# Value tiles of a gated recurrence brought to token layout by block transposes and transfers instead of TensorE transposes

## The chip, the cores and the metric

The kernel runs on one core of a Trainium2 chip. The metric is the device time of one execution in microseconds (us). A core has five engines that run their own instruction streams and meet at semaphores: PE (TensorE, matrix products into PSUM), DVE (VectorE), ACT (ScalarE), POOL (GpSimd) and SP (SyncE, which here only issues transfers). ACT issues transfers too, on a queue of its own.

## The reference

One layer of a hybrid encoder on 512 tokens of width 1024: a SwiGLU block, then a mixer with attention and a bidirectional gated recurrence side by side, then a second SwiGLU block. All in float32. The part that matters here:

```python
h = rmsnorm(x, mix_norm_g[l])
aq, ak, av, hq, hff, hfb, hi, hg, ga, gb = split_columns(h @ w_in[l])
y_attn = axial_gqa_attention(aq, ak, av, ...) @ w_branch_attn[l]
y_hgrn = hgrn2_bidirectional(hq, hff, hfb, hi, hg, ...) @ w_branch_hgrn[l]

# in the recurrence, v = hi, 8 heads of 64 channels, chunks of 32 tokens:
o_intra = einsum('bhnts,bhnse->bhnte', scores, v)
contrib = einsum('bhnsd,bhnse->bhnde', k * exp(b_last - b), v)
```

`hi` (the recurrence's values, 512 channels) comes out of the projection with channels on partitions, four tiles of 128 channels by 512 tokens. The two products above contract over tokens, so they want the values with tokens on partitions.

## The kernel before

The kernel is written out by hand for each engine, with semaphores between them; nothing is scheduled by a tool. Weights stream through in units of 128x1024 (512 KB). For a unit SP loads `raw` (two slots), ACT copies it to `w_hi` in the matmul's rounded type, DVE subtracts to get `w_lo` (four slots), and PE makes 24 matmuls of 128x512 (eight input tiles, each hi*hi, hi*lo and lo*hi) into one PSUM bank, alternating between two. DVE then evacuates the bank, multiplying by the token's norm factor `rs`.

The projection stage runs over `PROJ`, a list of 26 such units: attention v and k, four of q, then (before) four value tiles `hi`, four forget tiles `hf`, and so on. Every engine has a loop over this list with the same index i, and does in iteration i:

- PE (lines 1356 to 1379): unit i, once its weights are split (three units ahead) and the bank is read (unit i-2 evacuated). Behind the unit of a value tile, four transposes of 128x128 of `v_tmp` into PSUM bank 7 (line 1371). Then, from i = 9 on, the scores of attention item q = i - 9 (line 1329, two matmuls), which wait for `p_done` of item q-1.
- DVE (lines 1000 to 1037): for i from 10 on the reciprocal of the last item's sums; the evacuation of unit i (line 1026), for a value tile into `v_tmp`; from i = 9 on `attention_step` (line 967): block transposes of item q-1's probabilities (lines 962 and 965), then the two maxima of item q (line 974); then the split `w_lo` of unit i+3.
- ACT (lines 587 to 624): the scaling of item q-1's probabilities (line 564), the copy `w_hi` of unit i+3 (line 430), behind a value tile the copy of bank 7 to `v_h` (line 618), and the two exponentials of item q (line 558), which wait for the maxima.
- SP (lines 280 to 298): the weight loads, the swapped halves for the rotary embedding, and at i = 13 to 16 the transfers that replicate attention's v (line 295).

There is one `v_tmp` tile. Before, the attention value tile (i = 0) and the four `hi` tiles (i = 6 to 9) all go through it and through PE's transposes. `v_h` holds the result and is read first by `contributions(0)` of the recurrence (line 1449), after the projection stage. PE waits there for `vn_done`, the count of copies. Block transposes on DVE exchange rows and columns inside each 32x32 block; to bring the blocks themselves to their places, the kernel moves them by transfers. It does this already for x in the second SwiGLU block (`x_to_tokens`, line 448, issued by ACT).

Of the kernel before, what the change touches and what calls it, by code (L numbers as in the profile page):

```python
# [29 lines left out]
ACT = mybir.ActivationFunctionType  # L30
AX = mybir.AxisListType

P = 128
# [23 lines left out]
for _name, _count, _width in STREAMS:  # L57
# [3 lines left out]

PROJ = ([("av", 0), ("ak", 0)] + [("aq", t) for t in range(4)] + [("hi", t) for t in range(4)]
        + [("hf", h) for h in range(4)] + [("hq", t) for t in range(4)]
        + [("hf", h) for h in range(4, HH)] + [("hg", t) for t in range(4)])
V_TILES = {i: w for w, i in enumerate(i for i, (kind, _) in enumerate(PROJ) if kind in ("av", "hi"))}
FIRST_ITEM = 9
BLOCK = 32
BLOCKS = S // BLOCK  # L70
# [24 lines left out]
def build(nc, xT_in, up1, down1, proj, gates, branch, wout, up2, down2, mix_const, small_const, gains, gain_row, lb_logits, x_spill, out):  # L95


    with ExitStack() as ctx:
# [3 lines left out]
        def sem(name):  # L102
            return ctx.enter_context(nc.semaphore(name))
# [109 lines left out]
        lb_loaded, lb_exp, lb_ready = sem("lb_loaded"), sem("lb_exp"), sem("lb_ready")  # L213
        proj_read = sem("proj_read")
        vt_done, vn_done = sem("vt_done"), sem("vn_done")
        qsq_done, qms_done, qeps_done, qr_done = sem("qsq_done"), sem("qms_done"), sem("qeps_done"), sem("qr_done")
        cos_done = sem("cos_done")
        qn_done, rope_done = sem("qn_done"), sem("rope_done")
# [192 lines left out]
        def _(act):  # L411
# [138 lines left out]
                    split_hi(2)  # L550
            ffn(1)

            def exp_scores(q):
                for a in range(2):
                    act.wait_ge(nm_done, 2 * q + 1 + a)
                    if q:
                        act.wait_ge(pt_done, TURNS * q if a else TURNS * (q - 1) + 1)
                    A(prob[:, a, :], ps[:, 2 + a, :], ACT.Exp, bias=neg_max[:, q, a:a + 1],  # L558
                      accum_out=prob_sum[:, q, a:a + 1]).then_inc(p_done, 1)
# [27 lines left out]
            for i, (kind, t) in enumerate(PROJ):  # L587
                if i == 2:

                    act.wait_ge(lb_ready, 1)  # L590
                    A(lbt[:], lbt[:], ACT.Exp).then_inc(lb_exp, 1)
                if 3 <= i <= 7:
                    m = i - 3
                    act.wait_ge(qms_done, m + 1)
                    if m:
                        act.wait_ge(qn_done, m)
                    A(q_ms[:], ps[:, 4, :], ACT.Copy, bias=EPS).then_inc(qeps_done, 1)
                    act.wait_ge(qeps_done, m + 1)
                    A(q_rs[:], q_ms[:], ACT.Ln).then_inc(act_seq, 1)
                    act.wait_ge(act_seq, m + 1)  # L600
                    A(q_rs[:], q_rs[:], ACT.Exp, scale=-0.5).then_inc(qr_done, 1)
                if 0 <= i - FIRST_ITEM - 1 < ITEMS:
                    normalize_probs(i - FIRST_ITEM - 1)
                for n in {0: (0, 1), 1: ()}.get(i, (i,)):
                    split_hi(base + n + AHEAD)
                if i == 0:
                    rms_estimate(1)
                if kind in ("ak", "aq"):
                    m = i - 1
                    act.wait_ge(proj_read, i + 1 + BANK_CREDIT)  # L610
                    if m:
                        act.wait_ge(qms_done, m)
                    A(q_sq[:], qk[:, m, :], ACT.Square).then_inc(qsq_done, 1)
                w = V_TILES.get(i - 1)
                if w is not None:
                    act.wait_ge(vt_done, w + 1)
                    vt = ps[:, 7, :].rearrange("p (a b) -> p a b", b=P)
                    A(v_a[:] if w == 0 else v_h[:, :, P * (w - 1):P * w], vt, ACT.Copy).then_inc(vn_done, 1)
                q = i - FIRST_ITEM
                if q == Y_AT:  # L620
                    y_hi(0)
                    y_hi(1)
                if 0 <= q < ITEMS:
                    exp_scores(q)
            gate_base = BASE["gates"]


# [147 lines left out]
        def _(dve):  # L775
# [191 lines left out]
            def attention_step(q):  # L967

                if 0 <= q - 1 < ITEMS:
                    prob_blocks(q - 1)  # L970
                if 0 <= q < ITEMS:
                    for a in range(2):
                        dve.wait_ge(s_done, 2 * q + 1 + a)
                        V.reduce_max(neg_max[:, q, a:a + 1], ps[:, 2 + a, :], AX.X, negate=True).then_inc(nm_done, 1)  # L974
# [25 lines left out]
            for i, (kind, t) in enumerate(PROJ):  # L1000
                if i == 2:
                    lower_bound()
                if 3 <= i <= 7:
                    m = i - 3
                    dve.wait_ge(qr_done, m + 1)
                    link(newton(q_rs[:], q_ms[:], q_t[:]))
                    stt(qk[:, m, :], qk[:, m, :], gain[:, 33:34] if m == 0 else gq8[:], q_rs[:],
                        ALU.mult, ALU.mult).then_inc(qn_done, 1)
                    dve.wait_ge(qn_done, m + 1)
                if 0 <= i - FIRST_ITEM - 1 < ITEMS:  # L1010
                    inverse_sums(i - FIRST_ITEM - 1)
                if i != 1 and i < FIRST_ITEM:
                    split_lo(base + i + AHEAD)
                if i == 0:
                    split_lo(base + 1 + AHEAD)
                    rms_factor(1)
                if i - FIRST_ITEM == Y_AT:
                    y_lo(0)
                    y_lo(1)
                w = V_TILES.get(i)  # L1020
                if w:
                    dve.wait_ge(vt_done, w)
                dst = {"av": v_tmp[:], "hi": v_tmp[:], "ak": qk[:, 0, :], "aq": qk[:, min(1 + t, 4), :], "hf": forget[:, t, :],
                       "hq": hq[:, t % 4, :], "hg": hgate[:, t % 4, :]}[kind]
                dve.wait_ge(unit_done, base + i + 1 + W_CREDIT)
                tt(dst, ps[:, i % 2, :], rs[:], ALU.mult).then_inc(proj_read, 1)
                if 4 <= i <= 8:
                    m = i - 4
                    dve.wait_ge(mix_loaded, 16)
                    dve.wait_ge(qswap_done[m % 2], 64 * (m // 2 + 1))  # L1030
                    link(tt(q_t[:], q_swap[m % 2][:], c["sin"], ALU.mult))
                    dve.wait_ge(cos_done, m + 1)
                    tt(qk[:, m, :], q_cos[:, m % 2, :], q_t[:], ALU.add).then_inc(rope_done, 1)
                    dve.wait_ge(rope_done, m + 1)
                attention_step(i - FIRST_ITEM)
                if i >= FIRST_ITEM:
                    split_lo(base + i + AHEAD)
# [156 lines left out]
        def _(pe):  # L1194
# [137 lines left out]
            def weighted(w):  # L1332
                if w == 0:
                    pe.wait_ge(vrep_loaded, 16 * 2 * QUADS * QUADS)
                    pe.wait_ge(qeps_done, 5)
                    pe.wait_ge(vn_done, 5)
                else:
                    pe.wait_ge(yalo_done, 2 * w)
                pe.wait_ge(pt_done, TURNS * GROUP * (w + 1))
                for j in range(BLOCKS):  # L1340
                    piece = PIECE_OF[j]
                    for i in range(QUADS):
                        keys = slice(BLOCK * i, BLOCK * (i + 1))
                        for a, rows in enumerate(head_rows):
                            probs = prob_t1[piece][keys, j - PROB_PIECES[piece][0], :, :] if a else prob_t0[keys, j, :, :]
                            ins = T.matmul(ps[rows, Y_BANK + i, GROUP * BLOCK * w:GROUP * BLOCK * (w + 1)], v_rep[j // 8][keys, j % 8, rows],  # L1346
                                           probs.rearrange("p s c -> p (s c)"), start=j == 0, stop=j == BLOCKS - 1)
                ins.then_inc(pv_done, 1)
# [90 lines left out]
            def contributions(u):  # L1439
                pe.wait_ge(kn_done, u + 1)  # L1440
                if u == 0:
                    pe.wait_ge(vn_done, 5)
                if u >= 3:
                    pe.wait_ge(oeps_done, (u - 1) // 2)
                for n in range(NSUP):
                    j, tokens = n // 2, head_rows[n % 2]
                    for a, rows in enumerate(head_rows):
                        h = u // 2 * 2 + a
                        ins = T.matmul(ps[rows, 6 + n % 2, 0:S // 2].rearrange("p (e j) -> p e j", j=ST)[:, :, j],  # L1449
                                       k_nat[tokens, j, HD * a:HD * (a + 1)], v_h[tokens, j, HD * h:HD * (h + 1)], start=True, stop=True)  # L1450
                ins.then_inc(con_done, 1)
# [160 lines left out]
```

## Time and profile before

| | |
|---|---|
| median of 3 runs | 1132.91 us (lowest 1132.46) |
| the profiled execution | 1132.66 us |
| its span in the trace | 1130.9 us |
| PE busy | 1122.2 us, 99% of the span |
| PE weight loads (overlap PE) | 908.6 us, 80% |
| DVE busy | 628.8 us, 56% |
| ACT busy | 442.5 us, 39% |
| POOL busy | 81.5 us, 7% |
| chain that ended last | PE 98% |

The span is the time in the trace from the first to the last instruction; 1.8 us lie around it. One run of the three took 2531.6 us; it is left out. The chain that ended last is followed back from the last instruction, at each step to what released it. Matmuls overlap in the pipeline, so that the duration of one (0.39 us) is longer than its share (24 of them and the scores take 6.74 us).

### The profile page before, as it was taken

What the parts mean: (1) busy time and instruction counts of PE and PEld (TensorE: products, weight loads), DVE (VectorE), ACT (ScalarE), POOL (GpSimd) and SP (SyncE); (2) the same over time, 40 slices, a digit from 0 to 9 for tenths busy, and PEclk for the clock granted to TensorE, in tenths of its full rate; (3) what the DMA queues carried; (4) which work ended last, traced back from release to release, by engine and by line L of the source; (5) the groups of instructions that cost most, each with busy time, mean ns of one, the idle gap of its engine ahead of it and who ended that gap; (6) DMA issues with size and microseconds to landing.
All of it is one profiled execution on the core that took longest, in us unless ns stands there. A gap on an engine that the chain in (4) does not pass through costs nothing.

```text
span 1130.9 us, 16616 instructions
## 1 busy us (share of the span) xinstructions
PE 1122.2 (99%) x6359; PEld 908.6 (80%) x6359; DVE 628.8 (56%) x840; ACT 442.5 (39%) x658; POOL 81.5 (7%) x72
## 2 busy tenths in 40 slices
PE   9999999999999999999999999999999999999997
PEld 7888888888888777777788888888888888888886
DVE  6755555563332586647688767655555555542223
ACT  6423232232222444546856655534232323331223
POOL 0000000000000130000143320020000000000000
PEclk9999999999999999999999999999999999999999
DMA  6332322333322434212221222422244343332321
GB/s 198 124 111 75 111 92 93 108 113 103 103 95 74 172 110 133 75 57 75 76 79 57 74 76 93 168 93 93 79 126 121 91 120 108 119 110 93 99 88 75
DMA packets 51650, 114.78 MB, mean 101 GB/s; under 512 B 21904, under 2 KB 25104, under 8 KB 51344
## 3 DMA queue, kind: packets, MB, share of 16 engines
q1 hardware_dynamic: 32752, 105.16, 28.1%
q10 hardware_dynamic: 18848, 8.92, 2.7%
q8 instruction: 35, 0.57, 0.2%
q14 instruction: 15, 0.12, 0.0%
HBM read 105.41 MB, written 4.19 MB: 97 GB/s over the span
## 4 chain that ended last, share of the span: by engine, by line
PE 98%; DMA 1%; DVE 0%; ACT 0%; ACTq 0%; issue 0%; DVEq 0%
PE ps L1203 27%; PE ps L1205 27%; PE ps L1204 27%; PE ps L1229 4%; PE ps L1228 4%; PE ps L1230 4%; PE ps L1329 1%; PE ps L1346 1%; PE ps L1473 1%; DMA xT<-xT_dram 1%; PE ps L1466 0%; PE ps L1427 0%; PE ps L1449 0%; PE ps L1378 0%; PE ps L1416 0%; DMA raw<-up_dram 0%
## 5 line engine op out<-in xcount | busy, mean ns | idle before, releaser
L1203 PE MATMUL ps<-h_hi,w_hi 128*128 128x512 f32 x1024 | 407.3, 398 | 0.5 <-DVE w_lo L786 0.5
L1205 PE MATMUL ps<-h_hi,w_lo 128*128 128x512 f32 x1024 | 399.1, 390 | 0.0
L1204 PE MATMUL ps<-h_lo,w_hi 128*128 128x512 f32 x1024 | 398.8, 389 | 0.0
L786 DVE TENSOR_TENSOR w_lo<-raw,w_hi 128x1024 fp32r<-128x1024 f32 (+2 forms) x190 | 233.4, 1231 | 176.8 <-ACT w_hi L430 170.6
L430 ACT ACTIVATE w_hi<-raw 128x1024 fp32r<-128x1024 f32 (+1 forms) x182 | 194.7, 1080 | 182.8 <-PE ps L1205 74.3
L1203 PEld LDWEIGHTS ps<-h_hi,w_hi 128*128 128x128 f32 x1024 | 192.2, 188 | 55.8 <-issue 15.2
L1204 PEld LDWEIGHTS ps<-h_lo,w_hi 128*128 128x128 f32 x1024 | 192.3, 188 | 41.7 <-issue 2.9
L1205 PEld LDWEIGHTS ps<-h_hi,w_lo 128*128 128x128 f32 x1024 | 192.2, 188 | 40.6
L502 ACT ACTIVATE g_hi<-un 128x512 fp32r<-128x512 f32 (+1 forms) x44 | 27.8, 632 | 219.9 <-DVE un L786 219.9
L786 DVE TENSOR_TENSOR un<-ps,rs 128x512 f32<-128x512 f32 x44 | 30.4, 690 | 97.6 <-PE ps L1205 97.6
L1229 PE MATMUL ps<-w_hi,g_lo 128*128 128x512 f32 x176 | 68.5, 389 | 0.0
L1205 PE MATMUL ps<-g_hi,w_lo 128*128 128x512 f32 x176 | 68.5, 389 | 0.0
L1203 PE MATMUL ps<-g_hi,w_hi 128*128 128x512 f32 x176 | 68.5, 389 | 0.0
L1228 PE MATMUL ps<-w_hi,g_hi 128*128 128x512 f32 x176 | 68.5, 389 | 0.0
L1230 PE MATMUL ps<-w_lo,g_hi 128*128 128x512 f32 x176 | 68.5, 389 | 0.0
L1204 PE MATMUL ps<-g_lo,w_hi 128*128 128x512 f32 x176 | 68.5, 389 | 0.0
L786 DVE TENSOR_TENSOR g_lo<-un,g_hi 128x512 f32 (+1 forms) x44 | 30.5, 692 | 36.7 <-ACT g_hi L502 36.7
L438 ACT ACTIVATE sq<-xT 128x512 f32 (+1 forms) x16 | 10.1, 632 | 81.0 <-DVE xT L789 81.0
L558 ACT ACTIVATE prob<-ps,neg_max 128x512 f32<-128x512 f32 x32 | 21.7, 685 | 46.5 <-DVE neg_max L974 46.5
L1228 PEld LDWEIGHTS ps<-w_hi,g_hi 128*128 128x128 f32 x176 | 33.0, 188 | 6.9
L1205 PEld LDWEIGHTS ps<-g_hi,w_lo 128*128 128x128 f32 x176 | 33.0, 188 | 6.9
L1204 PEld LDWEIGHTS ps<-g_lo,w_hi 128*128 128x128 f32 x176 | 33.0, 188 | 6.9
(232 smaller groups left out, 1140.6 us busy)
## 6 DMA issues: line engine op xcount, KB each, us to landing
raw<-up_dram SPq DMA_DIRECT2D x86, 512.0 KB, 3.3
raw<-proj_dram SPq DMA_DIRECT2D x26, 512.0 KB, 3.3
raw<-down_dram SPq DMA_DIRECT2D x16, 704.0 KB, 4.0
raw<-down_dram SPq DMA_DIRECT2D x22, 512.0 KB, 3.3
raw<-gates_dram SPq DMA_DIRECT2D x16, 512.0 KB, 3.3
raw<-branch_dram SPq DMA_DIRECT2D x8, 512.0 KB, 3.3
raw<-wout_dram SPq DMA_DIRECT2D x8, 512.0 KB, 3.3
x_spill_dram<-xT ACTq DMA_DIRECT2D x1, 2048.0 KB, 7.1
```

The source lines that it names most:

```text
L430: A(w_hi[:, cst % 4, 0:width], raw[:, cst % 2, 0:width], ACT.Copy).then_inc(hi_done, 1)
L502: A(g_hi[:, 2 * it + q, :], un[:], ACT.Copy).then_inc(ghi_done, 1)
L558: A(prob[:, a, :], ps[:, 2 + a, :], ACT.Exp, bias=neg_max[:, q, a:a + 1], accum_out=prob_sum[:, q, a:a + 1]).then_inc(p_done, 1)
L786: return V.tensor_tensor(out, a, b, op)
L1203: T.matmul(ps[:, bank, :], w_hi[:, slot, cols], moving_hi(j), start=start and j == 0, stop=False)
L1204: T.matmul(ps[:, bank, :], w_hi[:, slot, cols], moving_lo(j), start=False, stop=False)
L1205: ins = T.matmul(ps[:, bank, :], w_lo[:, slot, cols], moving_hi(j), start=False, stop=stop and j == tiles - 1)
L1228: T.matmul(ps[:, bank, :], g_hi[:, j, rows], w_hi[:, slot, cols], start=first, stop=False)
L1229: T.matmul(ps[:, bank, :], g_lo[:, j, rows], w_hi[:, slot, cols], start=False, stop=False)
L1230: ins = T.matmul(ps[:, bank, :], g_hi[:, j, rows], w_lo[:, slot, cols], start=False, stop=end)
L1329: T.matmul(ps[:, 2 + a, :], qk[rows, 1 + t, P * qt:P * (qt + 1)], qk[rows, 0, :], start=True, stop=True).then_inc(s_done, 1)
L1346: ins = T.matmul(ps[rows, Y_BANK + i, GROUP * BLOCK * w:GROUP * BLOCK * (w + 1)], v_rep[j // 8][keys, j % 8, rows], probs.rearrange("p s c ...
```

## The change

Three things change together. The order of `PROJ`: the first four forget tiles now come at i = 6 to 9 and the value tiles at i = 10 to 13. The way of the value tiles to `v_h`: DVE transposes `v_tmp` in place by blocks of 32x32 (it waits for its own evacuation first), and ACT issues sixteen transfers, each of 32 partitions by four runs of 32 elements (16 KB), into `v_h`, behind the exponentials of its iteration. And the waits: the evacuation of the next value tile into `v_tmp` now waits until all transfers of the last have landed (`vh_loaded`), and PE's waits for `vn_done` of the value tiles become one wait for `vh_loaded` ahead of `contributions(0)`. PE's four groups of transposes and ACT's four copies are gone; attention's value tile keeps its own.

```diff
--- before.py
+++ after.py
@@ -61,10 +61,11 @@
 
 
 
-PROJ = ([("av", 0), ("ak", 0)] + [("aq", t) for t in range(4)] + [("hi", t) for t in range(4)]
-        + [("hf", h) for h in range(4)] + [("hq", t) for t in range(4)]
+PROJ = ([("av", 0), ("ak", 0)] + [("aq", t) for t in range(4)] + [("hf", h) for h in range(4)]
+        + [("hi", t) for t in range(4)] + [("hq", t) for t in range(4)]
         + [("hf", h) for h in range(4, HH)] + [("hg", t) for t in range(4)])
-V_TILES = {i: w for w, i in enumerate(i for i, (kind, _) in enumerate(PROJ) if kind in ("av", "hi"))}
+V_TILES = {0: 0}
+HI_AT = PROJ.index(("hi", 0))
 FIRST_ITEM = 9
 BLOCK = 32
 BLOCKS = S // BLOCK
@@ -213,6 +214,7 @@
         lb_loaded, lb_exp, lb_ready = sem("lb_loaded"), sem("lb_exp"), sem("lb_ready")
         proj_read = sem("proj_read")
         vt_done, vn_done = sem("vt_done"), sem("vn_done")
+        vblk_done, vh_loaded = sem("vblk_done"), sem("vh_loaded")
         qsq_done, qms_done, qeps_done, qr_done = sem("qsq_done"), sem("qms_done"), sem("qeps_done"), sem("qr_done")
         cos_done = sem("cos_done")
         qn_done, rope_done = sem("qn_done"), sem("rope_done")
@@ -550,6 +552,14 @@
                     split_hi(2)
             ffn(1)
 
+            def values_to_tokens(w):
+                act.wait_ge(vblk_done, w + 1)
+                blocks = v_tmp[:].rearrange("p (t j c) -> p t j c", j=QUADS, c=BLOCK)
+                for quad in range(QUADS):
+                    for to in range(QUADS):
+                        act.dma_start(v_h[BLOCK * to:BLOCK * (to + 1), :, P * w + BLOCK * quad:P * w + BLOCK * (quad + 1)],
+                                      blocks[BLOCK * quad:BLOCK * (quad + 1), :, to, :]).then_inc(vh_loaded, 16)
+
             def exp_scores(q):
                 for a in range(2):
                     act.wait_ge(nm_done, 2 * q + 1 + a)
@@ -615,13 +625,15 @@
                 if w is not None:
                     act.wait_ge(vt_done, w + 1)
                     vt = ps[:, 7, :].rearrange("p (a b) -> p a b", b=P)
-                    A(v_a[:] if w == 0 else v_h[:, :, P * (w - 1):P * w], vt, ACT.Copy).then_inc(vn_done, 1)
+                    A(v_a[:], vt, ACT.Copy).then_inc(vn_done, 1)
                 q = i - FIRST_ITEM
                 if q == Y_AT:
                     y_hi(0)
                     y_hi(1)
                 if 0 <= q < ITEMS:
                     exp_scores(q)
+                if kind == "hi":
+                    values_to_tokens(t)
             gate_base = BASE["gates"]
 
 
@@ -1017,9 +1029,8 @@
                 if i - FIRST_ITEM == Y_AT:
                     y_lo(0)
                     y_lo(1)
-                w = V_TILES.get(i)
-                if w:
-                    dve.wait_ge(vt_done, w)
+                if kind == "hi":
+                    dve.wait_ge(*((vh_loaded, 16 * QUADS * QUADS * t) if t else (vt_done, 1)))
                 dst = {"av": v_tmp[:], "hi": v_tmp[:], "ak": qk[:, 0, :], "aq": qk[:, min(1 + t, 4), :], "hf": forget[:, t, :],
                        "hq": hq[:, t % 4, :], "hg": hgate[:, t % 4, :]}[kind]
                 dve.wait_ge(unit_done, base + i + 1 + W_CREDIT)
@@ -1032,6 +1043,9 @@
                     dve.wait_ge(cos_done, m + 1)
                     tt(qk[:, m, :], q_cos[:, m % 2, :], q_t[:], ALU.add).then_inc(rope_done, 1)
                     dve.wait_ge(rope_done, m + 1)
+                if kind == "hi":
+                    dve.wait_ge(proj_read, i + 1 + BANK_CREDIT)
+                    V.transpose(v_tmp[:], v_tmp[:]).then_inc(vblk_done, 1)
                 attention_step(i - FIRST_ITEM)
                 if i >= FIRST_ITEM:
                     split_lo(base + i + AHEAD)
@@ -1333,7 +1347,7 @@
                 if w == 0:
                     pe.wait_ge(vrep_loaded, 16 * 2 * QUADS * QUADS)
                     pe.wait_ge(qeps_done, 5)
-                    pe.wait_ge(vn_done, 5)
+                    pe.wait_ge(vn_done, 1)
                 else:
                     pe.wait_ge(yalo_done, 2 * w)
                 pe.wait_ge(pt_done, TURNS * GROUP * (w + 1))
@@ -1439,7 +1453,7 @@
             def contributions(u):
                 pe.wait_ge(kn_done, u + 1)
                 if u == 0:
-                    pe.wait_ge(vn_done, 5)
+                    pe.wait_ge(vh_loaded, 16 * QUADS * QUADS * 4)
                 if u >= 3:
                     pe.wait_ge(oeps_done, (u - 1) // 2)
                 for n in range(NSUP):
```

On ACT, in the projection loop around the value tiles. Before, iterations 9 and 10 from the weight copy of the one to the exponentials of the other (`v_h` is the copy of the transposed tile out of PSUM, `prob` the attention item's probabilities):

```order
L430 ACTIVATE w_hi<-raw 128x1024 [waits unit_done,raw_loaded0]
L618 ACTIVATE v_h<-ps 128x4x128 [waits vt_done]
L558 ACTIVATE prob,prob_sum<-ps,neg_max 128x512 [waits nm_done] x2
L564 ACTIVATE prob<-prob,inv_sum 128x512 [waits inv_done]
L564 ACTIVATE prob<-prob,inv_sum 128x512
L430 ACTIVATE w_hi<-raw 128x1024 [waits unit_done,raw_loaded1]
L618 ACTIVATE v_h<-ps 128x4x128 [waits vt_done]
L558 ACTIVATE prob,prob_sum<-ps,neg_max 128x512 [waits pt_done,nm_done] x2
```

The changed kernel at the first value tile, iterations 10 and 11:

```order
L432 ACTIVATE w_hi<-raw 128x1024 [waits unit_done,raw_loaded1]
L568 ACTIVATE prob,prob_sum<-ps,neg_max 128x512 [waits pt_done,nm_done] x2
L560 DMA v_h<-v_tmp 32x4x32 [waits vblk_done]
L560 DMA v_h<-v_tmp 32x4x32 x15
L574 ACTIVATE prob<-prob,inv_sum 128x512 [waits inv_done]
L574 ACTIVATE prob<-prob,inv_sum 128x512
L432 ACTIVATE w_hi<-raw 128x1024 [waits unit_done,raw_loaded0]
L568 ACTIVATE prob,prob_sum<-ps,neg_max 128x512 [waits pt_done,nm_done] x2
```

The copies of `v_h` are gone, and sixteen issues stand between the exponentials of one iteration and the scaling, the weight copy and the exponentials of the next.

On DVE, one iteration of the same loop. Before, iteration 11, whose unit is a forget tile:

```order
L786 TENSOR_TENSOR forget<-ps,rs 128x512 [waits unit_done]
L962 STREAM_TRANSPOSE prob_t_67<-prob 128x16x32 [waits pn_done]
L965 STREAM_TRANSPOSE prob_t_0_68<-prob 128x4x32 [waits pn_done]
L965 STREAM_TRANSPOSE prob_t_4_69<-prob 128x5x32
L965 STREAM_TRANSPOSE prob_t_9_70<-prob 128x6x32
L965 STREAM_TRANSPOSE prob_t_15_71<-prob 128x32
L974 TENSOR_REDUCE neg_max<-ps 128x1 [waits s_done] x2
L786 TENSOR_TENSOR w_lo<-raw,w_hi 128x1024 [waits hi_done]
```

Now, iteration 11, whose unit is the second value tile:

```order
L798 TENSOR_TENSOR v_tmp<-ps,rs 128x512 [waits unit_done,vh_loaded]
L1048 STREAM_TRANSPOSE v_tmp<-v_tmp 128x512 [waits proj_read]
L974 STREAM_TRANSPOSE prob_t_67<-prob 128x16x32 [waits pn_done]
L977 STREAM_TRANSPOSE prob_t_0_68<-prob 128x4x32 [waits pn_done]
L977 STREAM_TRANSPOSE prob_t_4_69<-prob 128x5x32
L977 STREAM_TRANSPOSE prob_t_9_70<-prob 128x6x32
L977 STREAM_TRANSPOSE prob_t_15_71<-prob 128x32
L986 TENSOR_REDUCE neg_max<-ps 128x1 [waits s_done] x2
L798 TENSOR_TENSOR w_lo<-raw,w_hi 128x1024 [waits hi_done]
```

The evacuation waits for the transfers of the tile before (`vh_loaded`), and one block transpose stands between it and the attention item's work; the maxima and the weight split are queued behind both.

## Rows read from the trace of the kernel before

**Rows 1.** The page, busy us (share of the span) and instructions of each engine.

```profile
PE 1122.2 (99%) x6359; PEld 908.6 (80%) x6359; DVE 628.8 (56%) x840; ACT 442.5 (39%) x658; POOL 81.5 (7%) x72
```

**Rows 2.** Waits of PE over the whole span, the longest: us, times, longest.

```profile
PE ps L1315 <- POOL g_lo L316: 1.3, 1, 1.3
```

**Rows 3.** Busy us of the engines in a window; then clock, DMA share, GB/s.

```profile
434.00:474.00 40.00, 40.00 (x170) 28.12 (x169) 25.33 (x58) 21.53 (x40) 0.00 (x0) 1.00 0.32 98
```

**Rows 4.** Timeline of DVE, one iteration: start us, us, instruction, [idle before].

```profile
470.96 0.69 DVE L786 TENSOR_TENSOR hq<-ps,rs 128x512 f32<-128x512 f32 x1 [2.28 <-PE ps L1205]
471.57 0.70 DVE L962 STREAM_TRANSPOSE prob_t<-prob 128x512 f32<-128x512 f32 x1
472.20 0.85 DVE L965 STREAM_TRANSPOSE prob_t<-prob 128x128 f32<-128x128 f32 x4
472.97 1.24 DVE L974 TENSOR_REDUCE neg_max<-ps 128x1 f32<-128x512 f32 x2
...
477.70 0.69 DVE L786 TENSOR_TENSOR hq<-ps,rs 128x512 f32<-128x512 f32 x1 [2.28 <-PE ps L1205]
```

**Rows 5.** Timeline of ACT, the same iteration.

```profile
473.66 0.69 ACT L558 ACTIVATE prob<-ps,neg_max 128x512 f32<-128x512 f32 x1 [2.65 <-DVE neg_max L974]
...
474.33 0.68 ACT L558 ACTIVATE prob<-ps,neg_max 128x512 f32<-128x512 f32 x1
...
475.46 1.34 ACT L564 ACTIVATE prob<-prob,inv_sum 128x512 f32<-128x512 f32 x2 [0.36 <-DVE inv_sum L952]
```

**Rows 6.** Timeline of DVE, three evacuations, the first ahead of a transpose group.

```profile
436.80 0.69 DVE L786 TENSOR_TENSOR forget<-ps,rs 128x512 f32<-128x512 f32 x1 [3.20 <-PE ps L1205]
...
444.00 0.69 DVE L786 TENSOR_TENSOR forget<-ps,rs 128x512 f32<-128x512 f32 x1 [2.74 <-PE ps L1205]
...
450.75 0.69 DVE L786 TENSOR_TENSOR forget<-ps,rs 128x512 f32<-128x512 f32 x1 [2.28 <-PE ps L1205]
```

**Rows 7.** Tile v_h: ns min/median/max, first and last start.

```profile
L618 ACT ACTIVATE v_h<-ps x4: 597/598/599, 418.2 to 437.2; 128x512 f32<-128x512 f32 x4
L1449 PE MATMUL ps<-v_h,k_nat x256: 218/218/268, 575.9 to 663.1; 64*64 64x64 f32 x128
```

**Rows 8.** Line 448, ACT's transfers of x: issue ns, and time to landing.

```profile
L448 ACTq DMA_DIRECT2D x_tok<-xT x64: 592/632/744, 815.0 to 976.2; - x64
DMA to landing us min/median/max: 1.9/1.9/2.4
```

**Rows 9.** Timeline of ACT and its queue around four of these.

```profile
823.93 0.63 ACT L502 ACTIVATE g_hi<-un 128x512 fp32r<-128x512 f32 x1 [2.55 <-DVE un L786]
823.94 2.59 ACTq L448 DMA_DIRECT2D x_tok<-xT  x4
826.63 2.01 ACT L430 ACTIVATE w_hi<-raw 128x1024 fp32r<-128x1024 f32 x2 [2.07 <-issue]
```

**Rows 10.** Timeline of SP in the projection stage, and line 295 to landing.

```profile
431.54 5.06 SPq L295 DMA_DIRECT2D v_rep<-v_a  x8
...
443.00 5.07 SPq L295 DMA_DIRECT2D v_rep<-v_a  x8
...
DMA to landing us min/median/max: 1.8/1.9/3.9
```

**Rows 11.** Lines 287 and 298, SP's other transfers there: issue ns.

```profile
L287 SPq DMA_DIRECT2D q_swap<-qk x20: 507/590/618, 392.4 to 422.9; - x20
L298 SPq DMA_DIRECT2D raw<-proj_dram x26: 327/328/586, 333.7 to 516.2; - x26
```

**Rows 12.** Lines 414 and 256, loads issued by ACT and SP at the start.

```profile
L414 ACTq DMA_DIRECT2D raw<-up_dram x2: 413/434/456, 0.7 to 1.2; - x2
L256 SPq DMA_DIRECT2D xT<-xT_dram x6: 416/432/448, 1.2 to 6.6; - x6
```

**Rows 13.** Windows at the end: as rows 3; the last three are clock, DMA share, GB/s.

```profile
1124.00:1125.00 1.00, 0.35 (x2) 0.00 (x0) 0.79 (x4) 0.72 (x1) 0.00 (x0) 1.00 0.58 223
...
1127.00:1128.00 1.00, 0.00 (x0) 0.00 (x0) 0.71 (x1) 0.68 (x1) 0.00 (x0) 0.50 0.31 117
```

## The prediction

> **What bounds the kernel now.** I read the page's busy shares first, then who waits for whom on PE, then the projection stage alone. PE is busy 99% of the span [rows 1], and the longest that its matmuls waited for another engine was 1.3 us, once, at the very first of them (line 1315) [rows 2]. In 434 to 474 us, the stage that the change rewrites, PE is busy 40.00 of 40.00 us while DVE is busy 25.33 and ACT 21.53 [rows 3]. So PE's instruction stream is the kernel's length: what leaves PE shortens it by its own price, and what makes PE wait lengthens it by the wait.
>
> Next I looked at what feeds PE there. From i = 9 on each iteration of the projection loop also carries one attention item. One ordinary iteration starts with DVE's evacuation at 470.96 and the next at 477.70: 6.74 us. Of it DVE sat idle 2.28 us just before the evacuation, waiting for PE [rows 4]. ACT begins the two exponentials of the item at 473.66 after 2.65 us of idling [rows 5]. These two idle times are the whole cover that an addition on DVE or ACT has. There is a ring behind them: the scores of item q on PE wait for the exponentials of q-1, those wait for DVE's maximum, and that stands on DVE behind the evacuation of the same iteration.
>
> **What the change takes away.** Sixteen PE transposes (four behind each value tile) go. One group of four shows its price in the distance between evacuations: 436.80 to 444.00 is 7.20 us with a group, the next, 444.00 to 450.75, is 6.75 without [rows 6]. So 0.45 us a group, 1.8 us for four. The copies from PSUM to v_h on ACT, 0.6 us each [rows 7], go too; they stood in iterations where ACT waited for DVE or a load anyway, so they count nothing. DVE's waits for the PE transposes were covered in the same way, since PE never stood.
>
> **What it adds.** Each value tile now costs DVE one block transpose of 128x512 and ACT sixteen DMA issues, and the next value tile's evacuation waits on DVE until all sixteen have landed. The value tiles now stand at i = 10 to 13, where each iteration carries an attention item.
>
> The block transpose: 0.70 us, as the same form in [rows 4]; with the wait for the evacuation's own write I take 0.75 us. Alone it would fit in DVE's 2.28 us.
>
> The issues: no row shows this transfer, but two of the same kind, 32 partitions from SBUF to SBUF, stand near. ACT issues x_tok in four at 592 to 744 ns each, median 632 [rows 8], and four take 2.59 us, after which ACT's next instruction starts at 826.63, 0.1 us behind their end: ACT does nothing else while it issues [rows 9]. SP issues eight of v_rep in 5.06 us [rows 10]. Both give 0.64 to 0.65 us from one issue to the next. The lower bound is 0.51 us, the fastest q_swap issue [rows 11]; loads from HBM on both queues at the start were issued in 0.41 to 0.46 us [rows 12]. I take 0.65, the row on the same queue with the same 128-byte pieces. Sixteen then hold ACT 15 x 0.65 + 0.63 = 10.4 us, against a cover of 2.65 us in a period of 6.74. Landing: 1.9 us from the issue as a median, 3.9 at most [rows 8, 10].
>
> The chain from one value tile to the next, with time 0 at the start of its evacuation:
> - to the first exponential 473.66 - 470.96 = 2.70 us [rows 4, 5], plus the transpose 0.75: 3.45;
> - the second exponential starts 0.67 us later [rows 5], and the queue issues the first transfer as soon as an activation ahead of it has started (823.93 and 823.94 in [rows 9]): 4.1;
> - fifteen issues further the last one starts at 4.1 + 9.75 = 13.9, it lands at 15.8, and DVE starts the next evacuation at 15.9.
>
> Three such steps put the fourth value tile's evacuation at 47.7. Its sixteen issues end at 47.7 + 4.1 + 10.4 = 62.2. Then ACT still has to normalize the item that it left (0.62 us for the first half, then as much for the second, [rows 5]), DVE transposes its second half (0.8 us), takes the maximum (0.62 us) [rows 4], and ACT takes the exponential (0.69 us): 3.6 us with the handovers, 65.8.
>
> PE's side, with its ordinary 6.74 us an iteration and the same zero (end of unit 10): it comes to the scores of item 3, behind unit 12, at 13.5; they wait for an exponential of the second value tile at 15.9 + 4.2 = 20.1, so PE stands 6.6 us. The next two waits end at 36.0 and 51.9, each time 6.7 us of work after the last, 9.2 us of standing. The last ends at 65.8, after 7.1 us. Sum 32.1 us; the same as 65.8 less five ordinary iterations, 33.7. Behind it the loop is ordinary again, as DVE starts an iteration only when PE has ended a unit: nothing is won back, because PE was full before. The weight splits ahead (three units) and the recurrence, which first reads v_h at 575.9 us [rows 7], are not late.
>
> [...]
>
> **Sum.** 1132.66 us (the profiled execution; its span is 1130.9 and the median 1132.91, so all three agree within 0.2%) - 1.8 + 32.1 + 2.5 = 1165.5. With p for the step from issue to issue the stalls are 3 x (6.1 + 15p) + (7.8 + 16p) - 33.7 = 61p - 7.6. So everything hangs on p.
>
> **Rivals.**
> - The same chain, longer. For the first value tile ACT issues beside SP's v_rep sends (SP issues them until 448.1 in the trace, [rows 10]). If the two queues hold each other up, that group takes up to 5 us more; at the start both queues issued at 0.45 us side by side [rows 12], which speaks against it. A landing of 3.9 instead of 1.9 behind a weight load adds up to 3 x 2 = 6 us. A full iteration at half clock adds 4.2 over the sum. All at once: 1180.7. Chance 0.15.
> - Issues as cheap as the loads at the start, p = 0.45: 61 x 0.45 - 7.6 = 19.9, less 1.8, plus 2.5: 1153. At p = 0.33, the fastest weight load [rows 11], 12.5 us of stalls: 1146. For it: the new transfer has half the pieces of x_tok's. Against: v_rep and q_swap have still fewer pieces and cost as much. Chance 0.12.
> - Not slower: ACT's issues stay in its cover. It needs 61p - 7.6 to be at most the 1.8 us that PE saves, p = 0.15 us; the time would then be 1131. Nothing in [rows 8 to 12] comes near. [...] Chance 0.03.
>
> **How the numbers follow.** The forecast (p between 0.51 and 0.66) has 0.70. The range takes its own lower end, p = 0.51, 23.5 us of stalls and no clock loss, 1154.4, and the long case's end, 1181; that leaves out the two cheap cases. A measurement of this kernel tells about 2%, 22.7 us, from no change: slower by over 2% begins at 1155.6. The forecast and the long case lie beyond it but for the forecast's lowest edge (0.02): 0.83. Of the cheap case some lies beyond too (0.02): 0.85. Within 2%: 0.14. Faster by over 2% would need 22.7 us, and only 1.8 us leave PE: 0.01.
>
> **What would show it.** In the changed kernel's trace: (1) sixty-four ACT issues of v_h at 0.6 to 0.7 us each, in four blocks of about 10.4 us; (2) DVE's evacuations of v_tmp about 15.9 us apart, each ended by the landing of a v_h transfer; (3) PE standing four times, for 6.6, 9.2, 9.2 and 7.1 us, at the scores, released by ACT's prob; (4) the clock at 0.50 for a part of that stretch; (5) everything behind i = 15 moved by about 33 us and otherwise unchanged. The prediction is wrong if the issues are short or ACT goes on computing between them, or if PE stands at another place.

## The result and the profile after

The changed kernel takes 1166.85 us as a median (1165.87 to 1167.95) against 1132.92 us before: 1.0302 times as long, 95% interval 1.0288 to 1.0316. The prediction was 1165.5 us. The profiled execution took 1167.95 us, with a span of 1166.2 us.

Line numbers below are those of the changed kernel: the matmuls of a unit are L1217 to L1219 (L1203 to L1205 before), the scores L1343, the exponentials L568, the evacuations L798, the transfers of the value tiles L560.

Busy us, share of the span and instructions of each engine in the changed kernel:

```profile
PE 1133.6 (97%) x6343; PEld 914.1 (78%) x6343; DVE 631.3 (54%) x844; ACT 439.9 (38%) x654; POOL 81.5 (7%) x72
```

Beside [rows 1] PE has 16 instructions less, and yet is busy 11.4 us longer: it ran slower in part of the span (mean granted clock 0.984 beside 0.998). DVE has its four block transposes more and ACT its four copies less. That ACT's busy time fell by 2.6 us says nothing of its load, since issuing a transfer does not count as busy.

The waits of PE (us in total, times, longest):

```profile
PE ps L1343 <- ACT prob L568: 23.2, 4, 7.1
PE ps L1329 <- POOL g_lo L318: 1.3, 1, 1.3
PE ps L1487 <- issue: 0.9, 1, 0.9
PE ps L1217 <- DVE w_lo L798: 0.4, 1, 0.4
PE ps L1277 <- ACT h_hi L544: 0.2, 1, 0.2
```

The first row is new beside [rows 2]: four waits of the scores for ACT's exponentials. Line 560 alone, that is the 64 transfers, first their issues (ns), then who waited for them (us, times), then the landings:

```profile
L560 ACTq DMA_DIRECT2D v_h<-v_tmp x64: 592/622/1505, 439.7 to 497.4; - x64
...
  DVE v_tmp L798: 32.5, 3
...
DMA to landing us min/median/max: 1.8/1.9/3.6
```

The issues cost what those of x_tok in [rows 8] cost (median 0.62 us beside 0.63). The timeline of ACT from the second value tile's transfers to the third's:

```profile
455.58 0.68 ACT L568 ACTIVATE prob<-ps,neg_max 128x512 f32<-128x512 f32 x1
456.13 0.62 ACTq L560 DMA_DIRECT2D v_h<-v_tmp  x1
...
456.78 9.98 ACTq L560 DMA_DIRECT2D v_h<-v_tmp  x14
466.81 1.33 ACT L574 ACTIVATE prob<-prob,inv_sum 128x512 f32<-128x512 f32 x2 [10.46 <-issue]
468.05 1.04 ACT L432 ACTIVATE w_hi<-raw 128x1024 fp32r<-128x1024 f32 x1
471.42 0.69 ACT L568 ACTIVATE prob<-ps,neg_max 128x512 f32<-128x512 f32 x1 [2.33 <-DVE neg_max L986]
```

Between the last exponential and the scaling ACT computes nothing for 10.46 us, where an ordinary iteration has 2.65 us of idle time [rows 5]. The evacuations of the value tiles on DVE, each but the first ended by a landing:

```profile
435.69 0.69 DVE L798 TENSOR_TENSOR v_tmp<-ps,rs 128x512 f32<-128x512 f32 x1 [3.26 <-PE ps L1219]
...
451.50 0.69 DVE L798 TENSOR_TENSOR v_tmp<-ps,rs 128x512 f32<-128x512 f32 x1 [10.63 <-DMA v_h<-v_tmp]
...
468.01 0.69 DVE L798 TENSOR_TENSOR v_tmp<-ps,rs 128x512 f32<-128x512 f32 x1 [11.34 <-DMA v_h<-v_tmp]
...
483.68 0.69 DVE L798 TENSOR_TENSOR v_tmp<-ps,rs 128x512 f32<-128x512 f32 x1 [10.49 <-DMA v_h<-v_tmp]
...
512.11 0.69 DVE L798 TENSOR_TENSOR hq<-ps,rs 128x512 f32<-128x512 f32 x1 [4.69 <-PE ps L1219]
```

They lie 15.8, 16.5 and 15.7 us apart, where the evacuations of [rows 4] are 6.74 us apart. The scores of items 3 to 6 on PE:

```profile
455.73 2.74 PE L1343 MATMUL ps<-qk 64*128 64x512 f32 x4 [6.67 <-ACT prob L568]
...
472.25 2.74 PE L1343 MATMUL ps<-qk 64*128 64x512 f32 x4 [7.06 <-ACT prob L568]
...
487.92 2.74 PE L1343 MATMUL ps<-qk 64*128 64x512 f32 x4 [5.97 <-ACT prob L568]
...
501.81 2.74 PE L1343 MATMUL ps<-qk 64*128 64x512 f32 x4 [3.54 <-ACT prob L568]
```

The granted clock around the first and the last of them (columns as in [rows 3]):

```profile
454.00:455.00 1.00, 0.00 (x0) 0.00 (x0) 1.00 (x4) 0.10 (x1) 0.00 (x0) 0.50 0.00 0
...
459.00:460.00 1.00, 1.00 (x4) 0.81 (x3) 0.00 (x0) 0.00 (x0) 0.00 (x0) 0.50 0.84 241
...
461.00:462.00 1.00, 1.00 (x6) 0.83 (x5) 0.00 (x0) 0.00 (x0) 0.00 (x0) 1.00 0.04 3
...
502.00:503.00 1.00, 1.00 (x3) 0.81 (x4) 1.00 (x3) 0.64 (x3) 0.00 (x0) 0.50 0.00 0
...
507.00:508.00 1.00, 1.00 (x3) 0.77 (x3) 0.42 (x2) 0.64 (x3) 0.00 (x0) 0.50 0.00 0
...
509.00:510.00 1.00, 1.00 (x6) 0.82 (x5) 0.00 (x0) 0.74 (x1) 0.00 (x0) 1.00 0.90 352
```

PE comes out of each stall at 0.50 (in 455 to 456, 472 to 473, 488 to 489 and 502 to 503). The count in brackets is of the matmuls that touch the window, 3 to 4 in place of 6; in the timeline they start 0.43 us apart there (459.42, 459.85) and 0.23 us apart at 1.00 (461.38, 461.61). The clock is back at 1.00 some 5 to 7 us after the start of the scores (from 461, 478, 495 and 509 on). The fall that [rows 13] showed at the very end of the kernel before now happens four times in the middle.

### The profile page after: what moved, and what is told of

Same layout as the page of the kernel before. It is cut to its first block, busy times and chain, and to the rows that moved or that the text cites. A ratio compares the mean times of both kernels' runs of the same rounds, so it can differ in the third digit from the quotient of the medians.

```text
span 1166.2 us, 16645 instructions
## 1 busy us (share of the span) xinstructions
PE 1133.6 (97%) x6343; PEld 914.1 (78%) x6343; DVE 631.3 (54%) x844; ACT 439.9 (38%) x654; POOL 81.5 (7%) x72
## 3 DMA queue, kind: packets, MB, share of 16 engines
q10 hardware_dynamic: 28064, 9.97, 3.3%
## 4 chain that ended last, share of the span: by engine, by line
PE 92%; ACTq 3%; DVE 2%; DMA 1%; issue 1%; ACT 0%; DVEq 0%
PE ps L1217 26%; PE ps L1219 25%; PE ps L1218 25%; PE ps L1244 3%; PE ps L1243 3%; PE ps L1242 3%; ACTq L560 3%; PE ps L1360 1%; PE ps L1343 1%; PE ps L1487 1%; DMA xT<-xT_dram 0%; DMA v_h<-v_tmp 0%; PE ps L1463 0%; PE ps L1480 0%; PE ps L1441 0%
## 5 line engine op out<-in xcount | busy, mean ns | idle before, releaser
L1217 PE MATMUL ps<-h_hi,w_hi 128*128 128x512 f32 x1024 | 409.8, 400 | 0.4 <-DVE w_lo L798 0.4
L1219 PE MATMUL ps<-h_hi,w_lo 128*128 128x512 f32 x1024 | 401.0, 392 | 0.0
L798 DVE TENSOR_TENSOR w_lo<-raw,w_hi 128x1024 fp32r<-128x1024 f32 (+2 forms) x190 | 233.4, 1231 | 176.8 <-ACT w_hi L432 170.7
L1217 PEld LDWEIGHTS ps<-h_hi,w_hi 128*128 128x128 f32 x1024 | 193.9, 189 | 59.3 <-issue 18.4
L1219 PEld LDWEIGHTS ps<-h_hi,w_lo 128*128 128x128 f32 x1024 | 193.6, 189 | 41.3
L798 DVE TENSOR_TENSOR un<-ps,rs 128x512 f32<-128x512 f32 x44 | 30.4, 690 | 97.7 <-PE ps L1219 97.7
L1217 PE MATMUL ps<-g_hi,w_hi 128*128 128x512 f32 x176 | 68.5, 389 | 0.0
L1219 PE MATMUL ps<-g_hi,w_lo 128*128 128x512 f32 x176 | 68.5, 389 | 0.0
L798 DVE TENSOR_TENSOR g_lo<-un,g_hi 128x512 f32 (+1 forms) x44 | 30.5, 692 | 36.7 <-ACT g_hi L504 36.7
L1343 PE MATMUL ps<-qk 64*128 64x512 f32 x64 | 24.5, 765 | 23.2 <-ACT prob L568 23.2
L568 ACT ACTIVATE prob<-ps,neg_max 128x512 f32<-128x512 f32 x32 | 21.7, 684 | 45.2 <-DVE neg_max L986 45.2
L1219 PEld LDWEIGHTS ps<-g_hi,w_lo 128*128 128x128 f32 x176 | 33.0, 188 | 6.9
```

The source lines that it names most:

```text
L798: return V.tensor_tensor(out, a, b, op)
L1217: T.matmul(ps[:, bank, :], w_hi[:, slot, cols], moving_hi(j), start=start and j == 0, stop=False)
L1219: ins = T.matmul(ps[:, bank, :], w_lo[:, slot, cols], moving_hi(j), start=False, stop=stop and j == tiles - 1)
L1343: T.matmul(ps[:, 2 + a, :], qk[rows, 1 + t, P * qt:P * (qt + 1)], qk[rows, 0, :], start=True, stop=True).then_inc(s_done, 1)
```

## The experiments

The theory is that of the prediction: ACT is held for the length of sixteen issues inside a ring (exponentials of one item, scaling, block transposes and maximum on DVE, exponentials of the next) on which PE's scores depend, and with one buffer the next evacuation waits for the landing besides. The rivals: the new place among the attention items, the bytes and small pieces themselves, or the buffer alone.

**The order alone.** The kernel before, with value tiles at i = 10 to 13 and everything else kept.

```diff
-        ... + [("hi", t) for t in range(4)] + [("hf", h) for h in range(4)]
+        ... + [("hf", h) for h in range(4)] + [("hi", t) for t in range(4)]
```

> The kernel before with the order of the projection's units alone changed (value tiles at i = 10 to 13), PE's transposes and ACT's copies kept. Theory: the order costs nothing, since PE never stands and ACT's copy of 0.6 us fits its 2.65 us: 1132.9 us, within 0.5. Rival (the place among the attention items costs by itself): over 1140.

Measured: 1132.65 us, ratio 1.0000 (0.9991 to 1.0009). The order by itself costs nothing that these runs can show (0.1%).

**The old order with the new way.** The changed kernel with that line turned back.

> The changed kernel with the value tiles back at i = 6 to 9, ahead of the attention items but for the last; block transposes and ACT's transfers stay. Theory (the sixteen issues in a row on ACT are the cause, wherever they stand): the chain from tile to tile is still evacuation, block transpose, sixteen issues of 0.65 us and a landing, 13 us where nothing else is in it and about 17 us where DVE's q norm waits for ACT behind the issues; against 5.5 to 7 us of PE an iteration and three units of lookahead, some 29 us of stalls: about 1163 us, over 1150 in any case. Rival (it is the place among the attention items that costs, since there PE's scores depend on ACT in every iteration): 1131 to 1136 us.

Measured: 1175.03 us, ratio 1.0374 (1.0356 to 1.0391): slower even than the changed kernel, so the place among the attention items is not the cause; with the value tiles moved behind the forget tiles the changed kernel is 8 us faster. My figure was 12 us too low. The timeline of ACT in this kernel shows the issues of the first three tiles:

```profile
418.47 10.51 ACTq L560 DMA_DIRECT2D v_h<-v_tmp  x16
429.41 0.60 ACT L607 ACTIVATE q_ms<-ps 128x512 f32<-128x512 f32 x1 [17.49 <-issue]
...
438.73 10.60 ACTq L560 DMA_DIRECT2D v_h<-v_tmp  x16
449.43 1.06 ACT L432 ACTIVATE w_hi<-raw 128x1024 fp32r<-128x1024 f32 x1 [17.16 <-issue]
454.45 10.37 ACTq L560 DMA_DIRECT2D v_h<-v_tmp  x16
```

They are 20.3 and 15.7 us apart, where I had counted 17 and 13. Here the block transpose on DVE stands behind the rotary work of the iteration, and ACT's q norm and its weight copy stand behind the issues, with DVE's next evacuation behind both. So the ring holds more than I had counted: DVE waited 12.9 us for the q norm (`q_rs`) in the first step and 11.8 us for the weight copy in the second.

**A buffer for each tile.** The value tiles go to the four tiles of the q norm, which are free by then, and DVE waits for no landing. As these tiles are used again behind the projection loop, ACT now waits there for all 64 landings (the first line below); `v_buf` lists the four tiles.

```diff
+                act.wait_ge(vh_loaded, 16 * QUADS * QUADS * 4)
...
-                if kind == "hi":
-                    dve.wait_ge(*((vh_loaded, 16 * QUADS * QUADS * t) if t else (vt_done, 1)))
-                dst = {"av": v_tmp[:], "hi": v_tmp[:], ...
+                dst = {"av": v_tmp[:], "hi": v_buf[t % 4][:], ...
```

> The changed kernel with a buffer of its own for each value tile (the four tiles of the q norm, free by then), so that DVE never waits for a transfer to land; ACT issues sixteen in a row as before. Theory (ACT's issue time in the ring of the attention items): the ring is 10.4 us of issues + 3.5 us of scaling, transposes, maximum and exponential = 13.9 us an iteration in place of 15.9, so the stalls fall from 32 to 26 us and the time to 1160.7 us. Rival (the single buffer, i.e. DVE's wait for the landing, is the cause, 32.5 us of it in the trace): 1131 to 1136 us.

Measured: 1161.80 us, ratio 1.0257 (1.0239 to 1.0274). The groups of sixteen issues begin 14.2, 14.8 and 13.9 us apart in its trace, against 13.9 expected. DVE's 32.5 us of waiting for landings are gone by construction, and only 5 us came back. The largest wait in a list is not the price of what it waits for: behind it ACT was just as late.

**Eight and eight.** SP issues half of the transfers of each tile at the same time (in its iterations 15 to 18, ahead of v_rep's transfers); one buffer, all waits kept. `value_send(engine, k)` issues the k-th of the 64 transfers behind a wait for its block transpose.

```diff
+                        if 15 <= i <= 18:
+                            for k in range(16 * (i - 15) + 8, 16 * (i - 14)):
+                                value_send(sp, k)
...
-                    values_to_tokens(t)
+                    for k in range(16 * t, 16 * t + 8):
+                        value_send(act, k)
```

> The changed kernel with eight of the sixteen transfers of each value tile issued by ACT and the other eight by SP at the same time; one buffer, DVE's wait for all sixteen as before. Theory (61p - 7.6 is sixteen issues; with eight the period is 4.1 + 7 x 0.65 + 2.0 = 10.7 us and the tail 12.9): 11.3 us of stalls, 1.8 us saved, 0 to 3.5 us of clock: 1142 to 1146 us. Rival (the bytes and 128-byte pieces are the cost, not the issuing engine): unchanged at 1167. Rival (the buffer's wait whatever its length): over 1155.

Measured: 1144.84 us, ratio 1.0106 (1.0089 to 1.0123), inside the range expected. The evacuations in its trace stand at 435.26, 446.00, 457.48 and 468.72, so 10.7, 11.5 and 11.2 us apart against 10.7 expected. The same bytes in the same pieces cost 22 us less when eight issues stand in a row in place of sixteen.

**All on SP, one buffer.** ACT is free of them.

```diff
-                if kind == "hi":
-                    values_to_tokens(t)
...
+                            for k in range(16 * (i - 15), 16 * (i - 14)):
+                                value_send(sp, k)
```

> The changed kernel with all sixteen transfers of a value tile issued by SP in place of ACT, still one buffer and DVE's wait for the landing. ACT is free. Theory (with one buffer the issues of a tile stand between two evacuations on DVE, whoever issues them): 1.4 + 9.8 + 1.9 = 13.2 us from tile to tile and up to 16 us where SP also sends v_rep, so item 4's exponentials come at 49.6 us in place of about 27: 22.6 us of stalls, 1.8 saved, 0 to 3.5 of clock: 1154 to 1158 us. Rival (only ACT's occupation matters): 1131 us.

Measured: 1157.22 us, ratio 1.0215 (1.0199 to 1.0230). The timeline of DVE in this kernel:

```profile
435.51 0.69 DVE L798 TENSOR_TENSOR v_tmp<-ps,rs 128x512 f32<-128x512 f32 x1 [3.26 <-PE ps L1219]
...
448.71 0.69 DVE L798 TENSOR_TENSOR v_tmp<-ps,rs 128x512 f32<-128x512 f32 x1 [8.03 <-DMA v_h<-v_tmp]
...
465.83 0.69 DVE L798 TENSOR_TENSOR v_tmp<-ps,rs 128x512 f32<-128x512 f32 x1 [11.95 <-DMA v_h<-v_tmp]
```

The first step is 13.2 us, as worked out; the second is 17.1, where up to 16 was expected. Ahead of the second tile's transfers SP sends v_rep for 5.1 us (447.49 to 452.56), and one issue among the sixteen took 1.7 us. So each of the two bonds keeps most of the loss by itself: with only ACT's occupation left 29 us of 34 remain, with only the buffer's wait left 24, though these 24 hold SP's other sends too.

**Both bonds cut, on ACT.** Four buffers as above, and ACT issues four transfers in each iteration from 10 to 25. Same engine, same 64 issues; from the kernel with a buffer for each tile it differs only in where they stand.

```diff
-                if kind == "hi":
-                    values_to_tokens(t)
+                if i >= HI_AT:
+                    for k in range(4 * (i - HI_AT), 4 * (i - HI_AT + 1)):
+                        value_send(act, k)
```

> The changed kernel with four buffers, and ACT's 64 issues spread as four an iteration over i = 10 to 25, behind the exponentials. Same transfers, same engine, same count. Theory (only what passes ACT's idle 2.65 us in an iteration is paid, and 4 x 0.65 = 2.6 us does not): the ring is 6.1 us, below PE's 6.74, no stall; PE's transposes are saved: 1131.1 us. Rival (64 issues cost 64 x 0.65 less cover wherever they stand, or the landing traffic costs): over 1150.

Measured: 1132.50 us, ratio 0.9998 (0.9989 to 1.0007). The 34 us are gone with the count of issues unchanged, 29 of them by the spreading alone (1161.80 with sixteen in a row): what costs is their standing in a row. But the 1.6 us that the next run keeps are not there; the figure expected was 1.4 us too low. The first group of weighted sums still comes 2.06 us earlier than before (489.09 against 491.15), the second only 1.41 (549.37 against 550.78). The difference is lost at one place, the scores behind the iteration in which ACT also makes `ya_hi` (a part of attention's output):

```profile
509.59 1.79 PE L1343 MATMUL ps<-qk 64*128 64x512 f32 x4
```

They take 1.79 us in place of 1.13: the second two of the four matmuls wait for the second exponential. Before, this iteration left DVE 0.57 us of idle time ahead of the next evacuation in place of 2.28 [rows 4], and here DVE waits 4.72 us for `ya_hi` in place of 3.32. So four issues fit the idle time of an ordinary iteration, but not that of this one. More is lost behind the projection loop, where the trace shows ACT's first instruction:

```profile
547.20 1.28 ACT L586 ACT_TABLE_LOAD   x1 [1.72 <-DMA v_h<-q_t]
```

In the run on SP that instruction starts at 543.75 us, before at 545.50. Behind it ACT is busy 9.97 of 10 us (550 to 560), so what it starts late it ends late, and the first outputs of the recurrence come only 0.85 us earlier than before (583.51 against 584.36). That the wait for the last landing and the last issues did this second part is read from the trace and was not tried.

**Both bonds cut, on SP.** Four buffers; SP issues six transfers behind each weight load from i = 15 on.

```diff
+                        for k in range(max(0, 6 * (i - 15)), min(64, 6 * (i - 14))):
+                            value_send(sp, k)
```

> The changed kernel with four buffers, and the 64 transfers issued by SP, six behind each weight load from i = 15 on. Theory: SP has room, ACT gets its time back, the weight loads come 3.9 us later at most against two iterations of slack: 1131.1 us. Rival (SP is late with the weight loads in its first two iterations, where it also sends v_rep for 5 us): some us of stalls at PE behind w_lo, 1133 to 1140.

Measured: 1131.16 us against 1132.73, ratio 0.9986 (0.9977 to 0.9995): the fastest kernel of this study. The waits of PE in it:

```profile
PE ps L1328 <- POOL g_lo L328: 1.3, 1, 1.3
PE ps L1276 <- ACT h_hi L554: 0.6, 1, 0.6
PE ps L1486 <- issue: 0.6, 1, 0.6
PE ps L1216 <- DVE w_lo L799: 0.3, 1, 0.3
```

None is in the projection stage. What is left, 1.6 us, is the price of the sixteen transposes as far as the time shows it, against 1.8 in the prediction.

**The clock.** Matmuls of no use on PE in the time in which it stands, first with some room left, then as many as the stalls hold by the trace of the first (29, 34, 35 and 32).

```diff
+                for _ in range({12: 24, 13: 32, 14: 32, 15: 24}.get(i, 0)):
+                    T.matmul(ps[:, 7, :], h_hi[:, 0, 0:P], h_hi[:, 0, :], start=True, stop=True)
```

> The changed kernel with matmuls of no use on PE (24, 32, 32 and 24 of 128x512 into bank 7) ahead of the scores of items 3 to 6, in the time in which PE stands; the output is unchanged. It keeps PE's clock up and changes no wait. Theory (the clock costs 3.5 us behind the last stall and nothing behind the first three, which are hidden): 1163.4 us. If the clock costs nothing: 1166.9. If it costs at all four stalls (4 x 3.5): 1153. If the filler outlasts a stall: over 1166.9.

Measured: 1166.58 us, ratio 1.0295 (1.0278 to 1.0312), not the 1163.4 expected. PE still stood 1.9 us ahead of the last scores, and the granted clock was 0.50 for 3.4 us behind them (505.6 to 509.0). So this run could not decide.

> The changed kernel itself, unaltered, beside the next two on the same chip: 1166.9 us, as the measure for the run with more filler.

> As the filler run, with as many matmuls as the stalls hold by its trace (29, 34, 35 and 32 in place of 24, 32, 32 and 24), since there PE still stood 1.2, 0.7, 1.0 and 1.9 us and the granted clock fell behind the first and the last of these. Theory (in the changed kernel the clock costs 3.5 us behind the last stall): with the clock at 1.00 throughout, 3 us less than the unaltered kernel, 1163.9. If the clock is not what the 3.5 us are: no less than it.

Measured side by side: 1167.21 us (1166.21 to 1167.46) unaltered, 1167.05 us (1166.49 to 1168.01) with the full filler. No gain, against 3 us expected. In the trace of the full filler the clock behind the last stall stayed up:

```profile
505.14 1.79 PE L1343 MATMUL ps<-qk 64*128 64x512 f32 x4 [0.33 <-ACT prob L568]
```

```profile
507.00:508.00 1.00, 1.00 (x5) 0.82 (x6) 1.00 (x4) 1.00 (x2) 0.00 (x0) 1.00 0.79 233
```

From these scores to the next evacuation that waits for PE (512.64) it took 7.5 us. In the unaltered kernel it took 9.3 us in the run beside it (502.33 to 511.60) and 10.3 in the first, and 6.8 us in an ordinary iteration (470.86 to 477.70). So 1.8 to 2.8 us came back with the clock. The 0.7 us that stay are not the clock's. PE's weight loads for the scores, first in an ordinary iteration before, then here:

```profile
470.86 0.30 PEld L1329 LDWEIGHTS ps<-qk 64*128 64x128 f32 x4 [0.35 <-issue]
```

```profile
505.14 0.29 PEld L1343 LDWEIGHTS ps<-qk 64*128 64x128 f32 x2 [0.76 <-ACT prob L568]
505.81 0.29 PEld L1343 LDWEIGHTS ps<-qk 64*128 64x128 f32 x2 [0.38 <-ACT prob L568]
```

When PE stands at the scores, their second half waits for the second exponential, 0.67 us behind the first; in an ordinary iteration both are done. At 0.50 it is the same: in the old order with the new way one scores group that waits for no exponential takes 2.08 us (453.72), the stalled ones here take 2.74. Behind the first stall, where PE still stood 2.3 us, the clock did fall to 0.50 (459 to 460), but that one is hidden.

The time gained nothing because the last scores came 2.8 us later than beside it. ACT's transfers had become slower, as the rows of line 560 show, first of the unaltered kernel, then of the full filler:

```profile
L560 ACTq DMA_DIRECT2D v_h<-v_tmp x64: 592/622/1687, 439.8 to 498.0; - x64
...
DMA to landing us min/median/max: 1.8/1.9/3.5
```

```profile
L560 ACTq DMA_DIRECT2D v_h<-v_tmp x64: 592/622/2803, 439.5 to 500.8; - x64
...
DMA to landing us min/median/max: 1.8/1.9/4.5
```

The medians are equal; one issue took 2.8 us in place of 1.7, and one landing 4.5 in place of 3.5. They make up the delay: from the first evacuation of a value tile to the second it took 2.0 us more than beside it (18.05 against 16.04), from the fourth to the last scores 2.2 more (20.31 against 18.13), from the second to the third 1.1 less. Whether 130 more instructions on PE cause that is open. Of the 1.0 us by which the evacuation at 512.64 is late, most goes again later: the 0.9 us at L1487 are not in the filler's trace, and why is open too.

## Why the prediction was right

Point by point, with its own steps:

- Where PE would stand: at the scores, four times, released by ACT's exponentials. So it is in the trace, and four buffers, eight and eight and the spread issues each moved the time as this mechanism says, within 1.4 us of the figure or inside its range.
- The step from issue to issue, 0.65 us: 14 of them take 9.10 us in the last two groups and 15 take 9.75 us in the first, so 0.65 in each. Only the second group holds a long one.
- From evacuation to evacuation, 15.9 us: 15.8, 16.5, 15.7. The 16.5 holds one issue of 1.5 us.
- The last scores 65.8 us behind the first evacuation: 501.81 - 435.69 = 66.1.
- The standing times 6.6, 9.2, 9.2 and 7.1 us: 6.7, 7.1, 6.0 and 3.5. The sum is 23.2 in place of 32.1, so this sign holds for the first stall alone. The rest is not missing: between the stalls PE worked 9.5, 9.7 and 10.4 us in place of 6.7, since each began at a granted clock of 0.50 and its scores waited for the second exponential, and stood shorter for it. The prediction's standing times had no term for either.
- The clock: no run shows the 2.5 us of the sum, which was the author's estimate. In its place the runs showed 3.5 us: 10.30 us from the last stalled scores to the next evacuation against 6.84 in an ordinary iteration. With the clock kept up 7.50 remain, so 2.8 us of it came back with the clock; the other 0.7 is the wait for the second exponential, for which the prediction had no term. That the 2.5 came this close to the 2.8 is partly luck.
- The transposes, 1.8 us: 1.6 by the run on SP.
- The sum. The scores of item 6 came at 501.81 in place of 470.86, 30.95 us later, where 32.1 less 1.8 makes 30.3; with the 3.46 us behind them 34.4 us. The first group of weighted sums stands exactly that much later, 525.55 against 491.15. The profiled executions differ by 35.3 us; the rest is the wait of 0.9 us at L1487 for nothing that the profile shows, which the prediction did not have and whose cause is open. The medians differ by 33.9, the prediction said 32.8.

Each issue took 0.62 us beside 1.9 us to landing, and sixteen in a row 10.4 us; spread over SP, which computes nothing, the same 64 cost at most the 0.2 us that lie between 1.8 and 1.6. So one issue is a third of its landing time, and of a block of sixteen on a computing engine the issues weigh most: their 10.4 us are five times the one landing that shows behind them.

What the prediction had not weighed is that the same change costs nothing with two edits. Its formula counted ACT's time and the buffer's wait as one chain; the runs show that each alone keeps most of the loss.

## What to carry to other kernels

Price a transfer by its issuer too: n issues of 0.6 to 0.65 us hold the issuing engine n times that long, so a block of them belongs on an engine that computes nothing, or in portions that fit the idle time of the tightest iteration that they stand in. If a single buffer also makes the next producer wait for the last landing, moving the issues or adding a buffer alone brings little (here 10 and 5 us of 34); do both. A wait's length in a profile (32.5 us here) does not measure what its removal brings (5 us).

## What the hardware showed beyond this

- Single issues take much longer now and then. Beside a median of 0.62 us the longest was 1.5 us in the changed kernel, 1.7 in its second run, 1.9 and 2.8 with filler, and 1.7 on SP, with the medians unchanged (0.60 to 0.62). What causes them is not known here.
- SP and ACT issued side by side without holding each other up: in the run with eight and eight SP's first group (436.73 to 441.82) and ACT's (439.28 to 444.74) overlap, and the medians are 600 and 612 ns.
